# A dilated attention stage on one core: queries and keys of the two strided groups stored residue by residue

## The chip, the core and the metric

The kernel runs on one core of a Trainium2 chip. The core has a matrix engine (TensorE, PE in the rows; its weight loads are PEld), a vector engine (VectorE, DVE), an activation engine (ScalarE, ACT), a general engine (GpSimd, POOL) and DMA queues, all working beside one another and tied by semaphores. They share the on-chip memory SBUF; PE writes its products to PSUM. The metric is the device time of one execution of the whole program in microseconds, as a median over runs. Smaller is better.

## What is computed

Two transformer blocks in a row over 512 tokens of width 1024, in float32. The change touches one stage of the first block, the dilated attention of its second layer. It has 12 heads of 128 in three groups of four. Group 0 attends within a window of 128 tokens; group 1 to every 4th token in a window of 512, group 2 to every 16th in a window of 2048. The core of the reference:

```
DILATED_GROUPS = ((128, 1), (512, 4), (2048, 16))
...
    def to_blocks(t):
        t = t.reshape(B, L, dilation, Hg, D).transpose(0, 2, 3, 1, 4)
...
    scores = jnp.einsum('bdhnqe,bdhnke->bdhnqk', qb, kw, preferred_element_type=jnp.float32) * (D ** -0.5)
...
    p = jnp.exp(scores - m)
...
    out = jnp.einsum('bdhnqk,bdhnke->bdhnqe', p, vw.astype(jnp.float32)) / l
...
    alpha = jax.nn.softmax(lse, axis=2)
    o = (o * alpha[..., None]).reshape(B, S, ATTN_WIDTH).astype(u.dtype)
    return o @ w_out
```

Queries and keys are rotated by position first (`apply_rope`).

## The kernel before

**Weights.** All large products take their weights in two parts. A weight unit comes by DMA into a ring of four slots (SP's queue). ACT casts it to the high half of one of two slots of `w_split` (line 1121, `hi`), then POOL subtracts to get the low half (line 1613, `lo`). PE computes a unit by `unit` (lines 424 to 426): 8 chunks of three products each. ACT may cast unit n only when PE has used unit n - 2, since there are two slots. PE may start a unit when its low half is there.

**The attention stage.** Tokens lie along the free dimension, 512 columns, head features along the 128 partitions. It goes over four steps j = 0 to 3 (called heads 0 to 3 here; each takes one head of each group). For each there are six tiles of queries and keys: tile N = 6j + 2g is the query of group g, 6j + 2g + 1 its key. So tiles 0 to 5 belong to head 0, 6 to 11 to head 1, and so on; a tile is one weight unit (`qk_tile`).

A tile is rotated so: ACT copies it from PSUM to `raw` (line 1360, `take_raw`), POOL multiplies that by the cosines (line 1714, `times_cos`), DVE multiplies the PSUM values by the sines in two halves (line 2126), and one DVE add writes the sum to `QK` (line 2133). `QK` has two buffers of six tiles, used in turn by the heads. `raw` and `tsin` have two buffers.

In what order a token's columns lie in `QK` depends on the tile. Only the query of group 0 (N % 6 == 0) is written in another order than that of the tokens, by the view `by_query(0, ...)`: within each block of 128 the four residues one after the other, 32 columns each, so neighbouring tokens lie 32 words apart. The other five are written in order. `tokens(g, b)` is the slice of columns that make block b: 128 neighbouring ones for group 0, every 4th one for groups 1 and 2.

PE's order is written out by hand. Ahead of the loop it computes tiles 0 to 5. For each head j < 3 it computes tiles N, N+1, N+2 of the next head (N = 6(j+1)), the scores of head j (`attn_scores`, lines 678 to 704: group 0, then 1, then 2), tiles N+3 to N+5, then `attn_core` (lines 721 to 743): transposes of the weighted probabilities of groups 1 and 2, then of group 0 (line 727), and the products with the values (lines 736, 739, 742). In head 3 the order of the groups is 1, 0, 2, and the output projection `attn_out` 0 stands ahead of the scores, `attn_out` 1 to 3 behind them.

DVE's order, for a head j < 3: rotate tiles N and N+1; for each group mask the scores (line 2139) and reduce them to a maximum (line 2142); rotate tile N+2; `mix_tops` (lines 2150 to 2156); `weigh`, which waits for ACT's exponentials, forms the shares of the three groups, scales the probabilities of groups 1 and 2 (line 2174), copies 16 small pieces (line 2177) and scales those of group 0 (line 2180); rotate tiles N+3 and N+4; `ao_rest` (line 2187); rotate tile N+5. Line 2174 releases PE's transposes of groups 1 and 2, line 2180 those of group 0.

ACT's order behind the scores: exponentials of groups 0 and 1, then, when `mix_tops` is done, the exponential of the shares (line 1385), the cast of weight tile N+5, the exponentials of group 2, the copy of tile N+3, the cast for tile N+6 and the copy of tile N+4. In head 3 that wait stands ahead of the cast for `attn_out` 3. POOL's order: for each N the low half of tile N+2, then the cosine product of tile N.

Of the kernel before, what the change touches and what calls it, by code (L numbers as in the profile page):

```python
# [11 lines left out]
P = 128  # L12
# [81 lines left out]
def program(nc, a, out):  # L94
# [20 lines left out]
    with ExitStack() as ctx:  # L115
# [30 lines left out]
        gbias, eps_sq, start, r_tok = small[:, 4:6], small[:, 6:7], small[:, 8:12], small[:, 12:16]  # L146
# [14 lines left out]
        def views(used=0):  # L161
            at = [used]

            def take(*shape):
# [8 lines left out]
                if len(shape) == 3:  # L173
# [41 lines left out]
        SC_BANKS = [ps[:, 4:6].rearrange("p a (b n) -> p (a b) n", b=2), ps[:, 6].rearrange("p (b n) -> p b n", b=4),  # L215
                    ps[:, 7].rearrange("p (b n) -> p b n", b=4)]
# [81 lines left out]
        def score_order(j):  # L298

            return (0, 1, 2) if j + 1 < HPG else (1, 0, 2)  # L300


        def qk_bank(N):

            return 4 + N if N < 4 else N % 4

        def tokens(g, b):

            return slice(b * P, (b + 1) * P) if g == 0 else slice(b, T, RESIDUES)

        def by_query(g, v):

            if g == 0:
                return v.rearrange("p (b r m) -> p b m r", b=TT, r=RESIDUES)
            return v.rearrange("p (r b m) -> p b m r", r=RESIDUES, b=TT)

        def in_order(v):

            return v.rearrange("p (b m r) -> p b m r", b=TT, r=RESIDUES)
# [84 lines left out]
        def _(pe):  # L404
# [228 lines left out]
            def by_tokens(o, rr, per, width, c0, toks, first, last):  # L633

                for cc in range(per):
                    w = slice(cc * width, (cc + 1) * width)
                    uh, ul = us[:, 0, c0 + cc, toks], us[:, 1, c0 + cc, toks]
                    nc.tensor.matmul(o, uh, ws[:, 0, rr, w], start=first and cc == 0, stop=False)
                    nc.tensor.matmul(o, uh, ws[:, 1, rr, w], start=False, stop=False)
                    m = nc.tensor.matmul(o, ul, ws[:, 0, rr, w], start=False, stop=last and cc == per - 1)  # L640
                return m
# [10 lines left out]
            for g in range(GROUPS):  # L652
                base = 4 * (g % 2)
                for n in range(4):
# [11 lines left out]
                    for tt in range(TT):  # L666
                        if g == 2 and n == 0:
                            pe.wait_ge(s["av_ready"], tt + 1)
                        m = by_tokens(ps[:, base + tt], rr, 2, 512, 2 * n, tokens(g, tt), n == 0, n == 3)
# [9 lines left out]
            def attn_scores(j):  # L679
                last = j + 1 == HPG  # L680
                if last:
                    attn_out(0)
                else:
                    pe.wait_ge(s["qk_ready"], 6 * (j + 1))
                    if j:
                        pe.wait_ge(s["ao_lo"], 3 * j)
                for g in score_order(j):
                    if last:
                        pe.wait_ge(s["qk_ready"], 6 * j + 2 * g + 2)
                        pe.wait_ge(s["ao_lo"], 3 * (j - 1) + (3, 1, 2)[g])  # L690
                    q, k = QK[j % 2][:, 2 * g], QK[j % 2][:, 2 * g + 1]
                    for b in range(TT):
                        if g:
                            m = nc.tensor.matmul(SC_BANKS[g][:, b], q[:, tokens(g, b)], k[:, tokens(g, b)],
                                                 start=True, stop=True)
                            continue
                        qb = q[:, b * P:(b + 1) * P]
                        if b:
                            m = nc.tensor.matmul(SC_BANKS[0][:, b], qb, k[:, (b - 1) * P:(b + 1) * P], start=True, stop=True)
                        else:  # L700
                            for half in range(2):
                                m = nc.tensor.matmul(SC_BANKS[0][:, 0, half * P:(half + 1) * P], qb, k[:, 0:P],
                                                     start=True, stop=True)
                    m.then_inc(s["sc_ps"], 1)

            def attn_out(k):

                n, second = k // 8 * 4 + k % 4, k % 8 // 4
                rr, v, _ = split_use("attn_out", k)
                pe.wait_ge(s["w_lo"], v)  # L710
                rows = ps[:, n].rearrange("p (b m) -> p b m", b=TT)
                for c in range(6):
                    g, j, w = c % 3, 2 * second + c // 3, slice(c * P, (c + 1) * P)
                    if c % 3 == 0:
                        pe.wait_ge(s["ao_lo"], GROUPS * (j + 1))
                    oh, ol = ao_split[:, 0, g * HPG + j], ao_low(g, j)
                    nc.tensor.matmul(ps[:, n], ws[:, 0, rr, w], oh, start=not second and c == 0, stop=False)
                    nc.tensor.matmul(rows, ws[:, 0, rr, w], ol, start=False, stop=False)
                    m = nc.tensor.matmul(ps[:, n], ws[:, 1, rr, w], oh, start=False, stop=second == 1 and c == 5)
                used(m)  # L720
# [27 lines left out]
            for j in range(HPG):  # L748
                N = 6 * (j + 1)
                if j + 1 < HPG:  # L750
                    for n in range(3):
                        qk_tile(N + n)
                attn_scores(j)
                if j + 1 < HPG:
                    for n in range(3, 6):
                        qk_tile(N + n)
                else:
                    for k in range(1, 4):
                        attn_out(k)
                attn_core(j)  # L760
# [223 lines left out]
            for b in range(2):  # L984
                for k in range(4):
                    tt, g = divmod(b * 4 + k, 2)
                    m = nc.tensor.transpose(ps[:, 2 + b, k * P:(k + 1) * P],
                                            sC[:, tt, 4 * g:4 * g + 4].rearrange("p h n -> p (h n)"), ident[:])
# [98 lines left out]
            for j in range(DC):  # L1087
                b = 4 * (j % 2)
# [8 lines left out]
                for n, c in enumerate((4, 5, 6, 7) + UP_ORDER):  # L1097
# [6 lines left out]
                    m = nc.tensor.matmul(o, ws[:, 1, rr, w], up[:, c % 4], start=False, stop=n % 4 == 3)  # L1104
# [691 lines left out]
        def _(dve):  # L1796
# [325 lines left out]
            def rope(N):  # L2122
                dve.wait_ge(s["raw_ready"], N + 1)
                for lower in (0, 64):
                    src, dst = slice(lower, lower + 64), slice(64 - lower, 128 - lower)
                    nc.vector.tensor_tensor(tsin[dst, N % 2], ps[src, qk_bank(N)], sin_a[src], ALU.mult  # L2126
                                            ).then_inc(s["rope_sin"], 1)
                dve.wait_ge(s["rope_sin"], 2 * N + 2)
                dve.wait_ge(s["rope_cos"], N + 1)
                qk, x, y = QK[N // 6 % 2][:, N % 6], raw[:, N % 2], tsin[:, N % 2]  # L2130
                if N % 6 == 0:
                    qk, x, y = by_query(0, qk), in_order(x), in_order(y)
                nc.vector.tensor_tensor(qk, x, y, ALU.add).then_inc(s["qk_ready"], 1)

            def masked_max(j, g):
# [54 lines left out]
            for n in range(6):  # L2190
                rope(n)
            for j in range(HPG):
                N, more = 6 * (j + 1), j + 1 < HPG
                if more:
                    rope(N)
                    rope(N + 1)
                for g in score_order(j):
                    masked_max(j, g)
                if more:
                    rope(N + 2)  # L2200
                mix_tops(j)
                weigh(j)
                if more:
                    for n in range(3, 5):
                        rope(N + n)
                ao_rest(j)
                if more:
                    rope(N + 5)
# [288 lines left out]
            for j in range(DC):  # L2497
                b, x = 4 * (j % 2), 2 * (j % 2)
# [142 lines left out]
```

## Time and profile before

| | us |
|---|---|
| median of 3 runs | 2188.97 |
| lowest, highest | 2188.88, 2190.14 |
| span of the profiled execution, first to last instruction | 2187.2 |
| PE busy | 2145.5 (98%) |
| DVE busy | 1043.2 (48%) |
| ACT busy | 851.8 (39%) |
| POOL busy | 1172.4 (54%) |

Of the profiled execution the span is recorded; between it and the median of the runs lie 1.8 us. The mean granted clock of PE is 0.997 of full speed. Times in the rows are counted from the start of the span. The attention stage lies from about 770 to 1000.

Busy shares over the span say little for one stage. To see what a change in the stage is worth, one reads which instruction each engine waited for there, and the timeline, in which the idle time before an instruction and its releaser stand in brackets.

### The profile page before, as it was taken

To read this page: it belongs to the slowest core of one execution; us is meant where nothing else is said; L and a number is where in the kernel's file an instruction comes from. 1 tells how busy PE (TensorE), PEld (TensorE's weight loads), DVE (VectorE), ACT (ScalarE), POOL (GpSimd) and SP (SyncE) were. 2 spreads that over 40 slices of the span, in tenths; PEclk is the share of its full clock that TensorE was granted. 3 is DMA by queue.
4 is the path that set the end of the run, shared out by engine and by line. 5 is a ranking of instruction groups with operands and counts; after the bars stand their busy time and mean duration, and the time that the engine had idled before them with its cause. 6 is when DMAs were issued, how large, how long until landed. Compare 5 with 4: busy or idle time off the path is not lost. (4 is left out here: it accounts for less than half of the span.)

```text
span 2187.2 us, 28318 instructions
## 1 busy us (share of the span) xinstructions
PE 2145.5 (98%) x10458; PEld 1771.0 (81%) x10458; DVE 1043.2 (48%) x1483; ACT 851.8 (39%) x1210; POOL 1172.4 (54%) x635
## 2 busy tenths in 40 slices
PE   8999999999999999999999999999999999999997
PEld 6788878888888988888888888788767888888886
DVE  7766775422434037764431445463684344422433
ACT  6565654322333234444321233354664233322222
POOL 5777665554555464545554555483124555554552
PEclk9999999999999999999999999999999999999999
DMA  5212123332332332223332332323102223332331
GB/s 169 59 58 67 58 59 96 96 114 79 96 113 80 96 97 68 68 80 100 97 115 81 98 110 85 126 72 97 60 29 68 97 90 93 96 115 79 97 115 66
DMA packets 52822, 193.30 MB, mean 88 GB/s; under 512 B 6768, under 2 KB 7680, under 8 KB 52480
## 3 DMA queue, kind: packets, MB, share of 16 engines
q1 hardware_dynamic: 50688, 184.95, 27.5%
q10 hardware_dynamic: 2048, 7.19, 0.9%
q8 instruction: 56, 0.92, 0.2%
q14 instruction: 30, 0.25, 0.0%
HBM read 187.92 MB, written 4.19 MB: 88 GB/s over the span
## 5 line engine op out<-in xcount | busy, mean ns | idle before, releaser
L1613 POOL TENSOR_TENSOR w_split<-ring,w_split 128x1024 fp32r<-128x1024 f32 (+3 forms) x327 | 843.3, 2579 | 819.3 <-ACT w_split L1121 819.2
L1121 ACT CAST w_split<-ring 128x1024 fp32r<-128x1024 f32 (+3 forms) x327 | 356.3, 1090 | 991.2 <-PE ps L426 861.7
L424 PE MATMUL ps<-u_split,w_split 128*128 128x512 f32 x1768 | 704.7, 399 | 10.9 <-DVE u_split L1826 10.2
L426 PE MATMUL ps<-u_split,w_split 128*128 128x512 f32 x1768 | 690.4, 391 | 0.0
L425 PE MATMUL ps<-u_split,w_split 128*128 128x512 f32 x1768 | 690.0, 390 | 0.0
L424 PEld LDWEIGHTS ps<-u_split,w_split 128*128 128x128 f32 x1768 | 333.1, 188 | 88.1 <-issue 16.3
L426 PEld LDWEIGHTS ps<-u_split,w_split 128*128 128x128 f32 x1768 | 332.9, 188 | 70.8
L425 PEld LDWEIGHTS ps<-u_split,w_split 128*128 128x128 f32 x1768 | 333.2, 188 | 69.5 <-issue 3.1
L424 PE MATMUL ps<-hid,w_split 128*128 128x512 f32 x648 | 253.3, 391 | 4.3 <-DVE arena L2112 2.8
L426 PE MATMUL ps<-hid,w_split 128*128 128x512 f32 x648 | 252.2, 389 | 0.0
L425 PE MATMUL ps<-hid,w_split 128*128 128x512 f32 x648 | 252.1, 389 | 0.0
L1908 DVE TENSOR_TENSOR arena<-arena 128x512 f32<-128x512 f32 x66 | 162.0, 2454 | 66.1 <-ACT arena L1212 66.1
L1906 DVE TENSOR_TENSOR arena<-ps,rs_norm 128x512 f32<-128x512 f32 x66 | 45.7, 692 | 258.4 <-PE ps L426 236.4
L424 PEld LDWEIGHTS ps<-hid,w_split 128*128 128x128 f32 x648 | 121.7, 188 | 30.5 <-DVE arena L2112 3.2
L425 PEld LDWEIGHTS ps<-hid,w_split 128*128 128x128 f32 x648 | 121.7, 188 | 25.3 <-issue 0.2
L426 PEld LDWEIGHTS ps<-hid,w_split 128*128 128x128 f32 x648 | 121.6, 188 | 25.3
L1887 DVE TENSOR_TENSOR arena<-arena,ps 128x512 f32 x28 | 19.3, 688 | 187.5 <-PE ps L426 187.5
L1640 POOL TENSOR_TENSOR hid<-arena,hid 128x512 f32 (+1 forms) x66 | 85.3, 1292 | 5.8 <-ACT hid L1216 5.8
L1673 POOL TENSOR_TENSOR arena<-arena 128x256 f32<-128x256 f32 x70 | 63.3, 904 | 46.8 <-ACT arena L1236 46.8
L1912 DVE TENSOR_TENSOR arena<-ps,rs_norm 128x512 f32<-128x512 f32 x66 | 45.6, 691 | 81.5 <-PE ps L426 81.5
L2126 DVE TENSOR_TENSOR arena<-ps,mixer_consts 64x512 f32<-64x512 f32 x48 | 33.1, 689 | 79.9 <-ACT arena L1360 78.8
L1236 ACT ACTIVATE arena<-arena 128x1024 f32<-128x1024 f32 (+2 forms) x40 | 41.9, 1058 | 63.5 <-DVE arena L1953 56.2
(316 smaller groups left out, 2592.0 us busy)
## 6 DMA issues: line engine op xcount, KB each, us to landing
ring<-in_w_hgrn SPq DMA_DIRECT2D x32, 512.0 KB, 3.6
ring<-in_w_attn_qk SPq DMA_DIRECT2D x24, 512.0 KB, 3.6
ring<-in_w_merge SPq DMA_DIRECT2D x24, 512.0 KB, 3.3
ring<-in_w_gu0a SPq DMA_DIRECT2D x22, 512.0 KB, 3.6
ring<-in_w_gu0b SPq DMA_DIRECT2D x22, 512.0 KB, 3.5
ring<-in_w_gu1a SPq DMA_DIRECT2D x22, 512.0 KB, 3.6
ring<-in_w_gu1b SPq DMA_DIRECT2D x22, 512.0 KB, 3.5
ring<-in_w_gu2a SPq DMA_DIRECT2D x22, 512.0 KB, 3.5
```

The lines of the kernel that those rows point to most:

```text
L424: nc.tensor.matmul(ps[:, bank], ws[:, 0, r, w], act[:, 0, c], start=c == 0, stop=False)
L425: nc.tensor.matmul(ps[:, bank], ws[:, 0, r, w], act[:, 1, c], start=False, stop=False)
L426: m = nc.tensor.matmul(ps[:, bank], ws[:, 1, r, w], act[:, 0, c], start=False, stop=c == n - 1)
L1121: nc.scalar.copy(ws[:, 0, slot, 0:w], ring[:, r, 0:w]).then_inc(s["w_hi"], 1)
L1236: nc.scalar.activation(dv[:, lo:hi], dv[:, lo:hi], ACT.Exp).then_inc(s["dec_out"], 1)
L1613: nc.gpsimd.tensor_tensor(ws[:, 1, slot, 0:w], ring[:, r, 0:w], ws[:, 0, slot, 0:w].bitcast(F32), ALU.subtract).then_inc(s["w_lo"], 1)
L1640: nc.gpsimd.tensor_tensor(dst, gtmp[:, j % 2], src.bitcast(F32), ALU.subtract).then_inc(s["g_lo"], 1)
L1673: nc.gpsimd.tensor_tensor(x[:, :, 0], x[:, :, 0], kk[:, :, 0], ALU.mult)
L1906: nc.vector.tensor_tensor(gnorm[:, x], ps[:, 2 * x], rs[:], ALU.mult).then_inc(s["gate_norm"], 1)
L1908: nc.vector.tensor_tensor(sgate[:, x], sgate[:, x], gnorm[:, x], ALU.mult).then_inc(s["gate_silu"], 1)
L1912: nc.vector.tensor_tensor(gtmp[:, x], ps[:, 2 * x + 1], rs[:], ALU.mult).then_inc(s["up_norm"], 1)
L2126: nc.vector.tensor_tensor(tsin[dst, N % 2], ps[src, qk_bank(N)], sin_a[src], ALU.mult).then_inc(s["rope_sin"], 1)
```

## The change

Two edits. The add of the rotation now writes five of the six tiles of a head through `by_query`, all but the key of group 0. For groups 1 and 2 this view is another one than for group 0: the whole tile is ordered by residue, 128 columns for each residue, so neighbouring tokens lie 128 words apart in `QK`. The score products of groups 1 and 2 then take 128 neighbouring columns, `b * P` to `(b + 1) * P`, for queries and keys, where they took every 4th. Block b holds the same tokens in the same order as before. No instruction is added, removed or moved on any engine.

```diff
@@ attn_scores
                     for b in range(TT):
+                        qb = q[:, b * P:(b + 1) * P]
                         if g:
-                            m = nc.tensor.matmul(SC_BANKS[g][:, b], q[:, tokens(g, b)], k[:, tokens(g, b)],
-                                                 start=True, stop=True)
+                            m = nc.tensor.matmul(SC_BANKS[g][:, b], qb, k[:, b * P:(b + 1) * P], start=True, stop=True)
                             continue
-                        qb = q[:, b * P:(b + 1) * P]
@@ rope
                 qk, x, y = QK[N // 6 % 2][:, N % 6], raw[:, N % 2], tsin[:, N % 2]
-                if N % 6 == 0:
-                    qk, x, y = by_query(0, qk), in_order(x), in_order(y)
+                if N % 6 != 1:
+                    qk, x, y = by_query(N % 6 // 2, qk), in_order(x), in_order(y)
                 nc.vector.tensor_tensor(qk, x, y, ALU.add).then_inc(s["qk_ready"], 1)
```

## Rows read from the trace of the kernel before

**Rows 1.** PE's waits, 700 to 1100 us: line, releaser, total us, times, longest.

```profile
PE ps L717 <- POOL w_split L1613: 0.7, 1, 0.7
PE ps L727 <- DVE arena L2180: 0.7, 2, 0.3
```

**Rows 2.** Timeline of PE, head 0: start, us, engine, line, operation, count [idle before].

```profile
818.44 3.89 PE L694 MATMUL ps<-arena 128*128 128x128 f32 x16
821.98 0.58 PE L424 MATMUL ps<-u_split,w_split 128*128 128x512 f32 x1
...
838.51 1.03 PE L727 MATMUL ps<-ident_sb,arena 128*128 128x128 f32 x8
839.89 1.09 PE L727 MATMUL ps<-ident_sb,arena 128*128 128x128 f32 x8 [0.34 <-DVE arena L2180]
840.82 1.95 PE L736 MATMUL ps<-arena 128*128 128x128 f32 x16
842.61 0.61 PE L739 MATMUL ps<-arena 128*128 128x128 f32 x4
```

**Rows 3.** Timeline of DVE, head 0.

```profile
818.64 1.23 DVE L2139 SCALAR_TENSOR_TENSOR arena<-ps,mixer_consts 128x1024 f32<-128x1024 f32 x1 [1.60 <-PE ps L699]
...
825.26 0.69 DVE L2133 TENSOR_TENSOR arena<-arena 128x512 f32<-128x512 f32 x1
...
833.17 0.81 DVE L2169 TENSOR_TENSOR arena<-arena 128x12 f32<-128x12 f32 x1
834.02 1.22 DVE L2174 TENSOR_TENSOR arena<-arena 128x1024 f32<-128x1024 f32 x1
...
837.71 2.13 DVE L2180 TENSOR_TENSOR arena<-arena 128x1024 f32<-128x1024 f32 x1
```

**Rows 4.** Timeline of POOL, head 0.

```profile
830.30 2.40 POOL L1613 TENSOR_TENSOR w_split<-ring,w_split 128x1024 fp32r<-128x1024 f32 x1 [8.64 <-ACT w_split L1121]
832.66 1.30 POOL L1714 TENSOR_TENSOR arena<-arena,mixer_consts 128x512 f32<-128x512 f32 x1
834.40 3.10 POOL L1613 TENSOR_TENSOR w_split<-ring,w_split 128x1024 fp32r<-128x1024 f32 x1 [0.44 <-ACT w_split L1121]
837.47 1.28 POOL L1714 TENSOR_TENSOR arena<-arena,mixer_consts 128x512 f32<-128x512 f32 x1
```

**Rows 5.** Timeline of ACT, head 0.

```profile
831.68 0.56 ACT L1360 COPY arena<-ps 128x512 f32<-128x512 f32 x1
833.27 1.06 ACT L1121 CAST w_split<-ring 128x1024 fp32r<-128x1024 f32 x1 [1.03 <-PE ps L426]
```

**Rows 6.** Timeline of DVE: the add of tile 12, written with hops.

```profile
854.73 1.13 DVE L2133 TENSOR_TENSOR arena<-arena 128x512 f32<-128x512 f32 x1 [1.90 <-POOL arena L1714]
```

**Rows 7.** Timeline of DVE, from the end of head 2 to head 3.

```profile
925.34 1.58 DVE L2180 TENSOR_TENSOR arena<-arena 128x1024 f32<-128x1024 f32 x1
...
930.56 1.74 DVE L2133 TENSOR_TENSOR arena<-arena 128x512 f32<-128x512 f32 x1
...
937.41 0.69 DVE L2139 SCALAR_TENSOR_TENSOR arena<-ps,res_mask_sb 128x512 f32<-128x512 f32 x1 [1.02 <-PE ps L694]
...
939.15 1.23 DVE L2139 SCALAR_TENSOR_TENSOR arena<-ps,mixer_consts 128x1024 f32<-128x1024 f32 x1 [0.33 <-PE ps L699]
...
948.07 2.85 DVE L2174 TENSOR_TENSOR arena<-arena 128x1024 f32<-128x1024 f32 x1
...
953.39 1.23 DVE L2180 TENSOR_TENSOR arena<-arena 128x1024 f32<-128x1024 f32 x1
```

**Rows 8.** Timeline of POOL, heads 2 and 3.

```profile
929.92 1.83 POOL L1613 TENSOR_TENSOR w_split<-ring,w_split 128x768 fp32r<-128x768 f32 x1 [4.09 <-ACT w_split L1121]
...
948.01 1.82 POOL L1613 TENSOR_TENSOR w_split<-ring,w_split 128x768 fp32r<-128x768 f32 x1 [4.85 <-ACT w_split L1121]
```

**Rows 9.** Timeline of PE: transposes of head 2, first product of `attn_out` 3.

```profile
926.15 1.91 PE L727 MATMUL ps<-ident_sb,arena 128*128 128x128 f32 x16
...
949.88 0.50 PE L717 MATMUL ps<-ao_split,w_split 128*128 128x512 f32 x1 [0.73 <-POOL w_split L1613]
```

## What I expect of the change, and why

> **What bounds the kernel now.** I read first the list of waits of PE. In the 400 us from 700 to 1100, which hold the whole attention stage, PE waited 1.4 us in all: 0.7 for POOL's low halves of a weight slot at one place, 0.7 for DVE's line 2180 at two [rows 1]. So PE sets the pace, but the places where it waits say who is next, and how close. I therefore went to the timelines of head 0 (PE, DVE, ACT, POOL from 816 to 846), and laid them over one another. Heads 1 and 2 repeat them 43.8 and 87.6 us later.
>
> PE computes the scores (818.44 is the start of the two strided groups), then query and key tiles 9, 10 and 11, then at 838.51 the transposes of `attn_core` [rows 2]. Beside it runs a second chain. It begins on DVE at 818.64, when the scores of group 0 are there, and DVE has had 1.60 us of slack before it [rows 3]. From there DVE has no gap through the three masks, `rope(8)` and `mix_tops`; ACT's exponential follows, then ACT's high half of weight tile 11, POOL's low half of it (830.30 to 832.70), `weigh` on DVE, and line 2180 ends at 839.84 [rows 3 to 5]. PE meets this chain twice. Tile 11 starts at about 833.0 (three tiles take 16.53 us from 821.98 to 838.51, 5.51 each), 0.3 us after its low half; and the transposes of group 0 wait 0.34 us for line 2180 and start at 839.89 [rows 2]. So the chain on DVE, ACT and POOL is already as long as PE's own work. That decides the case.
>
> **The change, part by part.**
>
> *Score products of groups 1 and 2.* Each product is two records. The 16 records of line 694 with columns 4 apart take 818.44 to 821.98, 221 ns each; the 16 of line 736, the same 128x128 with neighbouring columns, take 840.82 to 842.61, 112 ns each [rows 2]. So PE saves 3.54 - 1.79 = 1.75 us a head, 7.0 in four. The first of these savings starts after group 0's scores, so the DVE chain does not start earlier for it: in heads 0 to 2 DVE reaches the masks of groups 1 and 2 without waiting for PE.
>
> *The adds of the rotation.* Four more of the six adds of a head (keys of group 0 stay as they are) now write with a hop at every element. An add that writes in a row takes 0.69, one that writes with hops (tile 12) 1.13 [rows 3, 6]: +0.43 to 0.44, 16 times, 6.9 us on DVE. The hop in the row is 32 words, the new one 128; no row shows that. Bounds: 0 (the plain add), and twice the row's surplus, 0.87. I take 0.43, since the row differs from the new case in nothing but the length of the hop. The Trainium skill (Vector Engine (DVE) Microarchitecture Reference, 5.2 Measured stream behaviour on trn2) says that a destination stepping 24 words at every element costs 2.50 ns a column, one hopping 4 KiB 1.71, a contiguous one 1.05. By the first the add would grow by 0.75 and the sum below would be +6.1, by the second by 0.34 and the sum would be +4.0; the row's 0.43 lies between them, as its hop does.
>
> Of the 16 adds most lie in gaps. On the chain are: that of tile 8 (14, 20 in the next heads), which stands between the masks and `mix_tops`, and in head 3 also those of tiles 22 and 23. Adds 9, 10 and 11 come after `weigh`, and the next scores come some 10 us later than they are done.
>
> *What tile 8's +0.43 does in head 0.* All of the chain behind it moves by 0.43: POOL's low half of tile 11 ends at 833.13 instead of 832.70. PE is there at 833.0 - 1.75 = 831.25, and waits 1.9 us. So the whole saving is gone before `attn_core`.
>
> *What the faster PE triggers.* DVE instructions with both inputs in SBUF and POOL's instructions do not overlap here: line 2169, 12 elements, took 0.81 because POOL's multiply (832.66, 1.30) was running, and ended with it; line 2174, started 0.06 us behind a POOL subtract in head 3, took 2.85 and ended 1.09 after it; a POOL subtract that met line 2174 took 3.10 [rows 3, 4, 7, 8]. Before, POOL's subtract for tile 12 started 0.44 after the multiply, since ACT's cast had waited 1.03 us for PE to finish tile 10 [rows 4, 5]; line 2174 at 834.02 came 0.38 before it and had the port. Now PE has finished tile 10 1.75 earlier, ACT casts as soon as it is free (832.24 + 0.43 = 832.67, done by 833.72), and the subtract follows the multiply at once, at 834.36. Line 2169 ends at 834.41, and line 2174 can start at 834.45, 0.1 after POOL, as in head 3. It ends 2.38 + 1.09 later than 834.36, at 837.83 instead of 835.24. The 16 copies take 2.47 to the start of line 2180, 840.29; POOL's next multiply is by then over, so line 2180 takes 1.23 [rows 7] and not 2.13, and ends at 841.52 instead of 839.84. PE's transposes start **1.68 us later** than before.
>
> *Sum.* Head 0 +1.68, head 1 the same. Head 2: the subtract has 768 columns (1.83) and would start at 921.98; line 2174 ends at 924.90, line 2180 at 928.61 instead of 926.92 (start 925.34, 1.58) [rows 7]; the transposes of group 0, 0.9 into the group at 926.15 [rows 9], move from 927.04 to 928.65, +1.6. Head 3: the add of tile 22 waits for POOL's subtract as before (929.92 + 1.83, now 1.6 later) and ends at 934.33 instead of 932.30 [rows 7, 8]; tile 23 adds 0.43, so DVE is at the first mask 2.46 later than it was free before; but there it had waited 1.02 and 0.33 for PE [rows 7], which comes 0.87 earlier now. That leaves 2.46 - 1.35, some 1.15, on the mask of group 0, and so on the high and low half of `attn_out` 3, for which PE already waits 0.73 [rows 9]. This 1.15 is what head 2 and 3 are worth together. Sum: 1.68 + 1.68 + 1.15 = **+4.5 us**. With an add that costs 0 more it is 1.25 + 1.25 - 0.2 = +2.3, with 0.87 more 2.12 + 2.12 + 2.4 = +6.7. Behind 960 nothing changes: PE is the bound there and carries the shift to the end. The span is 2187.2 and the median of the three runs 2188.97, 1.8 more, which I take as unchanged: 2188.97 + 4.5 = 2193.5.
>
> **Rivals.**
> - *DVE keeps the port* in front of the subtract. For it: in one row it is a matter of 0.1 us. Against: line 2174 lost in head 3 with 0.06 [rows 7, 8]. Line 2174 then takes 1.22, line 2180 waits for a multiply and ends at 840.4: +0.55, +0.55, and with head 3's gain of 0.45 set against head 2's 0.5 the sum is +1.1: 2190.1.
> - *The add is dearer*, through the hop of 128 words: up to +6.7, 2195.7. For it: nothing in this trace shows that hop. Against: 32 words cost 0.43. The page named above, by its nearest small step, would give 2195.1.
> - *PE's saving stays*: 2188.97 - 7.0 = 2182.0, faster. This holds if PE's arrivals alone set the stage. For it: PE waits 1.4 us in 400 [rows 1]. Against: the chain through DVE ends 0.3 before PE needs tile 11 and 0.34 after PE needs line 2180; it would have to lose 1.75 us a head, and nothing is taken out of it. It decides only where the chain has more than 1.75 us of slack, and in heads 0 to 2 it has none.
> - *The products don't get faster* (the 221 ns come from something else than the step). PE then does not arrive earlier, but tile 12's cast was done at 834.33 anyway, so POOL is ready as its multiply ends at 834.39, still before line 2174: again 1.68 a head, and 0.4 more in head 3: +4.9, 2193.9. So even a change that does not do what it says would be slower.
>
> **How the numbers follow.** The forecast 0.57, DVE keeps the port 0.20, dearer add 0.13, saving stays 0.05, products not faster 0.05. A measurement of this kernel tells about 0.2% from no change, 4.4 us, and the forecast's +4.5, with some 1.2 either way, lies on that edge: half of it on each side. Same: 0.28 + 0.20 + 0.02 = 0.50; slower: 0.29 + 0.13 + 0.03 = 0.45; faster 0.05. The range takes in the first three cases: 2190.1 less half a microsecond, to 2195.7.
>
> **What the profile after would show.** Line 694's successor: 16 records in 1.8 us and not 3.5. Adds of tiles 2 to 5 of each six at 1.12. PE's waits in the stage grown from 1.4 to about 12 to 13 us: three of about 1.9 at tiles 11, 17 and 23 for POOL's subtract, three of about 1.5 to 1.9 before the transposes of group 0 for line 2180, one of some 2 before `attn_out` 3. Line 2174 in heads 0 and 1 at about 3.4, in head 2 at 2.8, and not 1.22, and POOL's subtract beside it back at 2.4. I am wrong if line 2174 stays at 1.22 (second case), if the add shows another figure, or if the waits of PE do not grow (third rival).

## The result, and the profile after

The changed kernel takes 2194.31 us (median of 14 runs), the kernel before 2189.18 in the same series: ratio 1.0021, 95% interval 1.0014 to 1.0029. It is slower by 0.2%, 5.1 us between the medians where +4.5 was forecast, and most of that arises at the places that were forecast. The profiled execution has a span of 2192.1 us. Line numbers of the changed kernel are one lower than those of before from the score products on.

PE's waits from 700 to 1100 us (line, releaser, total us, times, longest), where before there were 1.4 us [rows 1]:

```profile
PE ps L424 <- POOL w_split L1612: 5.5, 3, 1.8
PE ps L716 <- POOL w_split L1612: 1.8, 1, 1.8
PE ps L726 <- DVE arena L2179: 1.7, 1, 1.7
```

Timeline of PE in head 0, beside [rows 2]:

```profile
817.60 1.95 PE L695 MATMUL ps<-arena 128*128 128x128 f32 x16
819.30 0.47 PE L424 MATMUL ps<-u_split,w_split 128*128 128x512 f32 x1
...
832.28 0.47 PE L424 MATMUL ps<-u_split,w_split 128*128 128x512 f32 x1 [1.83 <-POOL w_split L1612]
...
837.81 1.03 PE L726 MATMUL ps<-ident_sb,arena 128*128 128x128 f32 x8
840.57 1.09 PE L726 MATMUL ps<-ident_sb,arena 128*128 128x128 f32 x8 [1.72 <-DVE arena L2179]
```

From the first of the 16 score records to the next product it is 1.70 us, and not 3.54: PE does save its 1.8 us. Then it stands still for 1.83 before tile 11 and for 1.72 before the transposes of group 0. The other engines show why. DVE, beside [rows 3]:

```profile
824.39 1.09 DVE L2132 TENSOR_TENSOR arena<-arena 128x512 f32<-128x512 f32 x1
...
832.62 0.80 DVE L2168 TENSOR_TENSOR arena<-arena 128x12 f32<-128x12 f32 x1
833.45 3.36 DVE L2173 TENSOR_TENSOR arena<-arena 128x1024 f32<-128x1024 f32 x1
836.74 2.52 DVE L2176 COPY arena<-arena 32x1 f32<-32x1 f32 x16
839.29 1.23 DVE L2179 TENSOR_TENSOR arena<-arena 128x1024 f32<-128x1024 f32 x1
```

POOL, beside [rows 4], and ACT's cast for tile 12, beside [rows 5]:

```profile
829.78 2.36 POOL L1612 TENSOR_TENSOR w_split<-ring,w_split 128x1024 fp32r<-128x1024 f32 x1 [8.99 <-ACT w_split L1120]
832.10 1.29 POOL L1713 TENSOR_TENSOR arena<-arena,mixer_consts 128x512 f32<-128x512 f32 x1
833.35 2.39 POOL L1612 TENSOR_TENSOR w_split<-ring,w_split 128x1024 fp32r<-128x1024 f32 x1
```

```profile
831.63 1.04 ACT L1120 CAST w_split<-ring 128x1024 fp32r<-128x1024 f32 x1
```

The cast has no wait for PE in front of it any more, POOL's second subtract follows the multiply without a gap, and it starts at 833.35, 0.10 ahead of DVE's scaling of groups 1 and 2. That scaling takes 3.36 us where it took 1.22, and the one of group 0, free of POOL, 1.23 where it took 2.13.

To see where the time went I laid the two traces over one another instruction by instruction. This execution of the changed kernel is 0.7 us ahead from its first 10 us on and 0.84 ahead at 770, all before the code that was changed. From there (a plus is later; the last column is what the changed kernel loses in the part that ends at this row):

| | start before | start after | shift | added by the part up to here |
|---|---|---|---|---|
| scores of head 0, DVE mask | 818.64 | 817.80 | -0.84 | |
| scores of head 1, DVE mask | 862.48 | 863.14 | +0.66 | +1.50 |
| scores of head 2, DVE mask | 906.28 | 908.46 | +2.18 | +1.52 |
| `attn_out` 3, PE | 949.88 | 953.16 | +3.28 | +1.10 |
| last `ao_rest`, DVE | 960.03 | 964.90 | +4.87 | +1.59 |

From 960 to the end of the program the shift stays between 4.8 and 4.9, so nothing is won or lost behind the stage. The first three parts, 1.50, 1.52 and 1.10, are those predicted as 1.68, 1.68 and 1.15. The last was not predicted. The changed kernel's profile by stretches (us, PE busy, PEld busy, DVE, ACT, POOL, granted clock, DMA share, GB/s) shows it; in the kernel before the clock is 1.00 in all three:

```profile
876.00:884.00 8.00, 6.38 (x21) 5.14 (x22) 7.01 (x18) 2.49 (x7) 7.28 (x4) 0.79 0.23 66
...
922.00:928.00 6.00, 5.06 (x15) 4.07 (x16) 5.76 (x13) 1.59 (x3) 6.00 (x4) 0.72 0.20 67
...
952.00:960.00 8.00, 6.84 (x28) 5.60 (x29) 5.65 (x18) 1.02 (x3) 3.88 (x2) 0.79 0.15 49
```

Behind PE's waits of heads 1 to 3 the granted clock falls from 2.4 to 1.2 GHz (0.50 in 924 to 926 and in 954 to 956), for some 3.4 us each time by my estimate from the 0.79 over 8 us. Behind the two waits of head 0 it does not fall. In the timeline the products of `attn_out` 3 then come 0.43 us apart where they come 0.23 apart otherwise:

```profile
953.16 0.50 PE L716 MATMUL ps<-ao_split,w_split 128*128 128x512 f32 x1 [1.83 <-POOL w_split L1612]
953.50 0.39 PE L717 MATMUL ps<-ao_split,w_split 128*128 128x512 f32 x1
953.73 0.41 PE L718 MATMUL ps<-ao_split,w_split 128*128 128x512 f32 x1
953.96 0.60 PE L716 MATMUL ps<-ao_split,w_split 128*128 128x512 f32 x1
954.36 0.63 PE L717 MATMUL ps<-ao_split,w_split 128*128 128x512 f32 x1
954.79 0.63 PE L718 MATMUL ps<-ao_split,w_split 128*128 128x512 f32 x1
```

Eight such products at 0.20 more are 1.6 us. In heads 1 and 2 the lower clock costs nothing: PE would have waited for DVE anyway, and the wait before the transposes is gone instead (hence one such wait in the list, not three).

### The profile page after: what moved, and what is told of

The parts are those of the page before. It is cut to its first block and busy times, and to the rows that moved or that the text cites. A ratio compares the mean times of both kernels' runs of the same rounds, so it can differ in the third digit from the quotient of the medians.

```text
span 2192.1 us, 28318 instructions
## 1 busy us (share of the span) xinstructions
PE 2143.5 (98%) x10458; PEld 1765.8 (81%) x10458; DVE 1052.9 (48%) x1483; ACT 851.5 (39%) x1210; POOL 1172.6 (53%) x635
```

## The experiments

The times of whole executions of one kernel scatter by 3 to 4 us. In the eleven profiled executions the part outside the attention stage, which no edit touches, takes anything from 2001.8 to 2008.3 us. So besides each ratio I give the **stage**: from the start of tile 0's add to the start of the last `ao_rest` in the profiled execution. It is one execution for each kernel; the changed kernel has two, 0.04 us apart. The stage is 960.03 - 778.27 = 181.76 us in the kernel before, and 964.90 - 777.44 = 187.46 in the changed one, +5.70. What a head costs is read from one head's first DVE mask to that of the next.

| kernel | stage against before | ratio of times, 95% interval | median us (before beside it) |
|---|---|---|---|
| changed | +5.70 | 1.0021 (1.0014 to 1.0029) | 2194.31 (2189.18) |
| changed, again | +5.74 | 1.0022 (1.0013 to 1.0031) | 2193.71 (2189.25) |
| adds alone | +2.35 | 1.0004 (0.9995 to 1.0014) | 2189.95 (2190.07) |
| products alone | +2.53 | 1.0011 (1.0001 to 1.0020) | 2192.33 (2190.07) |
| changed, POOL held back | +1.50 | 1.0007 (0.9997 to 1.0017) | 2191.82 (2190.07) |
| changed, waits filled | +4.15 | 1.0024 (1.0014 to 1.0033) | 2194.50 (2190.07) |
| changed, two moves | -6.48 | 0.9968 (0.9956 to 0.9980) | 2182.57 (2189.25) |
| changed, three moves | -7.07 | 0.9968 (0.9957 to 0.9979) | 2182.60 (2189.25) |
| before, three moves | -1.09 | 0.9993 (0.9984 to 1.0002) | 2187.16 (2189.25) |
| changed, four moves | -5.75 | 0.9981 (0.9972 to 0.9990) | 2185.11 (2189.17) |

**The adds alone.**

```diff
-                            m = nc.tensor.matmul(SC_BANKS[g][:, b], qb, k[:, b * P:(b + 1) * P], start=True, stop=True)
+                            m = nc.tensor.matmul(SC_BANKS[g][:, b], q[:, tokens(g, b)], k[:, tokens(g, b)],
+                                                 start=True, stop=True)
```

> The changed kernel with the score products of groups 1 and 2 taken back to every 4th column; the adds still write by residue, so these products pair other tokens than the reference does. PE has no saving here. Theory (the chain DVE-ACT-POOL sets the stage): the add of tile 8 still moves it by 0.40, and POOL's subtract for tile 12, ready as the multiply ends, still comes about 0.05 to 0.1 before the scaling of groups 1 and 2: that scaling at 3.4 us, group 0's transposes 1.5 later a head, PE waits at tile 11 under 0.3 and before the transposes about 1.5; total +4 to +5 against the kernel before. Rival (only the earlier PE brings POOL in front): the scaling stays at 1.22 and the adds cost 0.4 a head, +1 to +1.5 in all.

Here the rival was right in heads 0 and 1: the scaling stayed at 1.22, and heads 0 and 1 cost 0.34 and 0.40 more, no more than the surplus of one add. In head 2 the theory was right, with 2.81. The stage, +2.35, lies between the two forecasts; the ratio, 1.0004, can't be told from 1. Timelines of DVE and POOL of this run, head 0 and then head 2:

```profile
833.75 1.22 DVE L2174 TENSOR_TENSOR arena<-arena 128x1024 f32<-128x1024 f32 x1
...
922.11 2.81 DVE L2174 TENSOR_TENSOR arena<-arena 128x1024 f32<-128x1024 f32 x1
```

```profile
833.76 3.46 POOL L1613 TENSOR_TENSOR w_split<-ring,w_split 128x1024 fp32r<-128x1024 f32 x1
...
922.00 1.84 POOL L1613 TENSOR_TENSOR w_split<-ring,w_split 128x768 fp32r<-128x768 f32 x1
```

In head 0 DVE starts 0.01 ahead of POOL and POOL's subtract is held up to 3.46; in head 2, where ACT's cast is shorter (768 columns), POOL starts 0.11 ahead and DVE is held up. Whichever of the two starts first goes through in these rows, and a tenth of a microsecond in the start is worth 1.6 us on DVE.

**The products alone.**

```diff
-                if N % 6 != 1:
-                    qk, x, y = by_query(N % 6 // 2, qk), in_order(x), in_order(y)
+                if N % 6 == 0:
+                    qk, x, y = by_query(0, qk), in_order(x), in_order(y)
```

> The changed kernel with the adds of groups 1 and 2 taken back to writing in a row; the products take neighbouring columns, so they pair other tokens than the reference does. PE saves 1.75 us a head, the adds cost what they did. Theory: POOL gets in front of the scaling by the earlier PE alone: 3.4 us for the scaling, transposes of group 0 1.1 to 1.25 later in heads 0 to 2, head 3 gains 0.2 to 0.5; +2 to +3 against the kernel before, PE waits of 1.4 at tiles 11, 17, 23, and perhaps 1 to 1.5 more where PE's clock falls behind them. Rival (PE's saving reaches the end when the adds are cheap): -5 to -7.

As expected by the theory: with the adds back at 0.69, the scalings still took 3.37, 3.37 and 2.81, PE waited 1.48 before tile 11 and 1.72 before group 0's transposes, and the stage grew by 2.53 with the clock at 1.00 all through it. DVE, POOL and PE of this run, head 0:

```profile
835.30 3.37 DVE L2173 TENSOR_TENSOR arena<-arena 128x1024 f32<-128x1024 f32 x1
```

```profile
835.19 2.40 POOL L1612 TENSOR_TENSOR w_split<-ring,w_split 128x1024 fp32r<-128x1024 f32 x1
```

```profile
842.41 1.09 PE L726 MATMUL ps<-ident_sb,arena 128*128 128x128 f32 x8 [1.72 <-DVE arena L2179]
```

PE had 7 us less to do, nothing else was touched, and the stage became longer. The earlier PE alone puts POOL in front.

**POOL held back.**

```diff
+                if N % 6 == 4 and N >= 10:
+                    pool.wait_ge(s["p_norm"], 2 * (N // 6 - 1) + 1)
                 lo("attn_qk", N + 2) if N + 2 < 24 else lo("attn_out", N - 22)
```

> The changed kernel; POOL waits for the scaling of groups 1 and 2 of the head before it takes the low half of tile 12 (18, attn_out 0). One wait more on POOL, nothing else. Theory (the port order is worth 1.0 of each head's 1.5): scaling back to 1.22, group 0's scaling at about 2.3 since it now meets the multiply, transposes 0.4 to 0.6 later than in the kernel before instead of 1.5; total 2 to 3 below the changed kernel, near +2 against before (the clock's part stays). Rival (the loss is the adds' 0.4 alone and POOL's place does not matter): no difference to the changed kernel, +4.5 to +5.5.

The scaling was back at 1.22, that of group 0 at 2.32. DVE and POOL of this run, head 1:

```profile
882.25 1.23 DVE L2175 TENSOR_TENSOR arena<-arena 128x1024 f32<-128x1024 f32 x1
```

```profile
883.56 2.39 POOL L1612 TENSOR_TENSOR w_split<-ring,w_split 128x1024 fp32r<-128x1024 f32 x1 [1.37 <-DVE arena L2175]
```

Head 1 cost 0.50 more than in the kernel before, where in the changed kernel it cost 1.52. So the order of two instructions between POOL and DVE is 1.0 of a head's 1.5, as expected. The stage was 4.20 shorter than in the changed kernel, but not all of that is the order: in this execution the clock fell in head 0 (0.79 in 836 to 844, and head 0 cost 1.19) and not at `attn_out` 3, where it had cost 1.6. Against the execution with the waits filled (below), whose clock stayed at 1.00, the order is worth 4.15 - 1.50 = 2.65 of the stage, with the 0.7 that the clock cost in head 0 still counted against it. The ratio is 1.0007 against 1.0021; the intervals just overlap.

**The waits filled with work.** `fill` issues eight products of 128x512 into a bank that is about to be overwritten.

```diff
+                if N in (11, 17, 23):
+                    fill(qk_bank(N), 8)
                 used(unit("attn_qk", N, us, qk_bank(N)))
...
                     for k in range(1, 4):
+                        if k == 3:
+                            fill(3, 8)
                         attn_out(k)
```

> The changed kernel; PE does eight products of 128x512 more (1.8 us, thrown away) where it waited 1.83 us: before tiles 11, 17, 23 and before attn_out 3. Nothing else is changed, and PE's useful work starts no earlier. Theory (the clock fell because of the waits, and cost 1.6 behind attn_out 3, nearly nothing in heads 1 and 2, where PE waits again): granted clock 1.00 all through 860 to 965, 1.3 to 1.7 us less than the changed kernel. Rival (the lower clock has another cause, or costs nothing): same time as the changed kernel, clock 0.94 to 0.96 again. If the fill itself delays PE, up to +0.3 a place.

In the profiled execution the clock stayed at 1.00 through the stage, and the stage was 1.55 shorter than the changed kernel's, both as expected. The ten runs show no gain: 1.0024 against 1.0021. They don't exclude one either, since 1.5 us are 0.07% and the intervals reach 0.07 to 0.1% to either side. The profiled execution as a whole was no shorter than the changed kernel's (2192.8 against 2192.1): in it the clock was 0.95 in 1500 to 1600, where the profiles of the changed kernel and of before have 0.97. So where the lower clock lay and what it cost is shown (1.6 us at `attn_out` 3). That the waits brought it on rests on this one execution, with 1.83 and 1.72 us of waiting in head 0 of the changed kernel against it, where the clock stayed up. And it is not shown that avoiding it there shortens the program.

**The changed kernel again.**

> The changed kernel once more, unchanged, beside the three that follow: +4.5 to +5.5 against the kernel before, and in its trace again 3.4, 3.4, 2.8 us for the scaling of groups 1 and 2 in heads 0 to 2 and 1.83 us of PE waiting at tiles 11, 17 and 23. Where in the program the granted clock falls may differ from the first profile; if it falls elsewhere, the attention stage is about 1.5 us shorter than there, +4.1 instead of +5.7 against the kernel before.

The stage is the same to 0.04 us. The clock stayed at 1.00 in head 1 this time and fell in heads 2 and 3, so the lower clock at `attn_out` 3 came in both executions. Both waits of head 1 then stand in the timeline, 1.82 and 1.71 us: the head costs the same either way (1.53 and 1.52). The medians are 4.5 us apart in this series.

**Two moves.** If the saving was lost only to the chain through DVE, ACT and POOL, then shortening that chain must bring it back. ACT casts tile N+5 before it waits for `mix_tops`, and DVE rotates tile N+2 after `mix_tops`, where it had been idle 2.84 us.

```diff
@@ ACT
                     exps(j, 0)
                     exps(j, 1)
+                    qk_weights(N + 5)
...
                 if more:
-                    qk_weights(N + 5)
                     exps(j, 2)
@@ DVE
+                mix_tops(j)
                 if more:
                     rope(N + 2)
-                mix_tops(j)
                 weigh(j)
```

> The changed kernel with two moves that shorten the chain beside PE: ACT casts weight tile N+5 before it waits for the tops of the shares, and DVE rotates tile N+2 behind the tops and not ahead of them. Theory (PE's saving was lost only to this chain): no wait at tiles 11, 17, 23; DVE takes the port before POOL's subtract for tile 12 (scaling 1.22), group 0's scaling still waits 0.9 for the multiply; transposes of group 0 1.5 earlier a head than in the kernel before, the stage 4 to 5 shorter than before, 2184.5 to 2186. Rival (the products' saving is small in itself or the adds on DVE cost PE time directly): within 2 us of the kernel before.

More than expected: 2182.57 us, 0.3% below the kernel before, where 2184.5 to 2186 was expected. PE no longer waits at tiles 11, 17 and 23. The scalings are as worked out (1.23 and 2.12), and PE waits 0.35 before the transposes in heads 0 and 1, none in head 2. What I had set too low is the gain of a head: I let the transposes come 1.5 earlier, and they came 1.92 earlier in head 0 (839.09 in a stage that began at 779.39, against 839.89 and 778.27), and 1.95 more in head 1.

**Three moves, on either kernel.** POOL also waits for the scaling of group 0 (the edit of the run with POOL held back, with `+ 2` for `+ 1`).

> The same two moves, and POOL also waits for the scaling of group 0 before it takes the low half of tile 12 (18, attn_out 0), so both scalings on DVE run alone. Theory: transposes never wait, each of heads 0 to 2 gives 1.75 to 2.1, head 3 about 0.9: the stage 6 to 7 us shorter than before, time 2182 to 2184, 11 us under the changed kernel: faster than both by 0.3%. Rival (POOL's later work delays tile 12 or the adds of tiles 10 and 11, and so the next scores): a new wait of PE there, and 2 us or more of this lost.

> The kernel before with the same three moves: products at every 4th column, adds in a row. Theory (before, PE set the pace but for 1.4 us of waits): the stage 0.7 to 1.4 us shorter than before, no more, so the three moves alone are worth 1 us and the products' columns the other 5 to 6 once the chain is out of the way. Rival (the moves are what brings the gain, the columns nothing): as fast as the same moves with the change.

With the change: both scalings at 1.23 in heads 0 to 2, no wait of PE at tiles 11, 17, 23 or before a transpose, and the stage 7.07 shorter. A head gives 2.5, more than the 1.75 to 2.1 expected. Without the change the same three moves give 1.09, and their ratio can't be told from 1. The difference, 5.98, is what the change is worth once nothing stands behind it. An estimate from the rows comes near: four times the 1.84 of the score products are 7.4, and PE waits 1.4 more in the stage than without the change (2.1 for 0.7), which leaves 6.0. The third move is worth 0.6 in the stage and nothing in the times. PE's waits in the stage with the change and three moves:

```profile
PE ps L716 <- POOL w_split L1612: 2.1, 2, 1.8
```

**A fourth move.** It takes up that last wait.

```diff
                     exps(j, 2)
+                    hi("attn_out", 3)
...
-                    for k in range(3, 6):
+                    for k in range(4, 6):
                         hi("attn_out", k)
```

> The changed kernel with the three moves (cast of tile N+5 ahead of the wait, rotation of tile N+2 behind the tops, POOL behind group 0's scaling) and a fourth: in head 3 ACT casts attn_out 3 before it waits for the tops of the shares. Theory (the last wait of PE in the stage, 1.85 us for that low half, is the same chain again): the wait is gone, the scaling of groups 1 and 2 in head 3 no longer meets that subtract (1.2 instead of 2.83 us), the stage another 1.6 to 1.9 shorter, 2180.5 to 2181.5. Rival (the wait moves to the transposes of head 3, since the scalings end late): less than 0.5 gained.

The rival was right, and more so: the wait went from `attn_out` 3 to the transposes of head 3 and grew to 2.6 us, and the stage is 1.3 longer than with three moves. The earlier subtract now lies beside the 16 small copies of `mix_tops`. DVE and POOL of this run:

```profile
935.94 4.36 DVE L2152 COPY arena<-arena 32x2 f32<-32x2 f32 x16 [0.83 <-ACT arena L1365]
```

```profile
938.25 1.84 POOL L1613 TENSOR_TENSOR w_split<-ring,w_split 128x768 fp32r<-128x768 f32 x1 [2.51 <-ACT w_split L1120]
```

The copies take 4.36 us for 2.75 to 2.80 in every other head and run, in none of which POOL works beside them: 1.6 more, near the subtract's own 1.84. The scaling of group 0 then ends 1.6 later in the stage than with three moves. The other thing expected failed too: the scaling of groups 1 and 2 took 2.86 and not 1.2, since POOL's next subtract, for `attn_out` 4, starts 0.06 ahead of it (941.75 and 941.81). It is the change under study once more: an instruction made earlier meets another engine's and holds it up.

## Why the prediction held, and where it did not

*What bounds the stage.* Right. PE set the pace before, but the second chain was as long, and PE's saving turned into waits at the two places named: 1.83 us before tile 11 (1.9 worked out), 1.72 before group 0's transposes (1.5 to 1.9 expected).

*The score products.* 1.75 us a head was worked out; 3.54 - 1.70 = 1.84 came.

*The adds.* 0.43 for a hop of 128 words, taken from the hop of 32: 1.09 us for 0.69, so 0.40. So the rival with a dearer add fell. The Trainium skill (Vector Engine (DVE) Microarchitecture Reference, 5.2 Measured stream behaviour on trn2) has 2.50 ns a column for a step of 24 words, 1.71 for a hop of 4 KiB and 1.05 for a plain write. My estimate from its 1.05 and the measured 0.40 / 512 puts the hop of 128 words at about 1.83, between the two and nearer the second.

*The port.* Right with its numbers: the subtract 0.10 us ahead of the scaling, the scaling 3.36 (3.38 worked out) and 2.81 in head 2 (2.82), the scaling of group 0 at 1.23. The price of the rival in which DVE keeps the port was right as well: 0.55 for a head, 0.50 in head 1 with POOL held back.

*The sum.* 1.68 + 1.68 + 1.15 = 4.5 was worked out, 1.50 + 1.52 + 1.10 = 4.1 came. The term that was mis-sized is the head: the add of tile 8 costs 0.03 less, the copies behind it begin only 0.32 later after its start than before, and DVE's scaling began 0.27 later after the chain's start, where I had 0.43. The step that is missing is the clock, 1.59 us at `attn_out` 3; with it the stage grew by 5.7. The medians of the runs differ by 5.1, between the two, and by 4.5 in the second series; 2194.31 lies inside 2189.6 to 2195.7. That the sum came so near the runs is in part luck: it was 0.4 too high in the terms that it had and lacked one of 1.6. Two slips in it are small: 2.46 - 1.35 is 1.11 and not 1.15, and 2.12 + 2.12 + 2.4 is 6.6 and not 6.7.

*PE's waits.* 12 to 13 us in the stage were expected, 9.0 came (5.5 + 1.8 + 1.7). Those at tiles 11, 17 and 23 and at `attn_out` 3 are there; of the three before the transposes only head 0's is, since in heads 1 and 2 the lower clock filled the time.

*The chances.* I gave 0.50 to no difference that could be told and 0.45 to slower, taking 4.4 us as the least that the runs can tell. The interval reaches only 0.08% to either side, some 1.7 us, so +4.5 could be told from nothing.

*The rival "the products don't get faster".* Its price was wrong. I wrote that POOL would come first even then, since its subtract was ready as the multiply ended. The run with the adds alone has DVE first, by 0.01 and 0.02 us, in two of three heads, and its stage costs 2.35, not 4.9. A step that turns on some hundredths of a microsecond between two engines can't be settled from a trace of another kernel; it should have been given two prices.

*The rival "PE's saving stays".* Wrong for this kernel. With the chain shortened most of it stays: 5.98 us.

*The expectation for the fill.* Its stage came out as expected in the trace of one execution, its gain does not show in the runs. What sets how often and where the clock falls stays open.

## What to carry to other kernels

An engine that waits 1.4 us in 400 can still be a bound that another chain shares: look at how soon before each of its starts the thing that it waits for was ready (here 0.3 us), and not at its waits alone. A saving on it was worth no more than that slack here, and what it triggered earlier made the stage longer than it was. Shorten the other chain first, or in the same change: this edit went from +0.2% to -0.3% with two lines moved, while three such moves without the edit gave 0.07%, which the runs can't tell from nothing.

## What the runs showed of the hardware that I had not expected

- A wait of PE of 1.83 us at `attn_out` 3 was followed in both profiles of the changed kernel by 1.2 GHz (in the first for eight products, 0.43 us apart and not 0.23, 1.6 us in all); one of 1.84 us there in the kernel with two moves was not (clock 1.00 in 944 to 956).
- DVE's 16 copies of 32x2 elements, one input each, took 4.36 us the one time that a POOL subtract ran beside them, and 2.75 to 2.80 otherwise. The 16 copies of 32x1 elements took the same 2.51 us beside a subtract (835.16 in the kernel before, beside the 834.40 of [rows 4]) and without (832.48 in the kernel with four moves). Before, I had counted only instructions with two inputs in SBUF among those that wait for POOL.
- A writing hop of 128 words costs as much as one of 32 within 0.04 us (1.09 and 1.13 for 512 columns).
